# Moving the experts' down-weight loads from SyncE's DMA queue to ScalarE's, in a hybrid decoder step

## The chip, the cores and the metric

One core of one Trainium2 chip runs the whole kernel. The time is device microseconds of one execution, as a median over runs. Engines are TensorE (PE, its weight loads PEld), VectorE (DVE), ScalarE (ACT), GpSimd (POOL) and SyncE (SP). SyncE and ScalarE can each start DMA transfers on a queue of their own; all transfers are carried out by the core's 16 DMA engines.

## The reference

One layer of a decoder for 256 prompt tokens and 8 decode tokens (264 in all, width 1024). Two attention mixers and a merge come first, then the mixture of experts, on which this case turns. Cut to that:

```
def moe_ffn(x, norm_ffn, w_router, b_router, w_gu, b_gu, w_down, b_down):
    xn = rms_norm(x, norm_ffn)
    logits = (xn @ w_router) + b_router
    top_v, top_e = lax.top_k(logits, TOP_K)          # 4 of 32 experts
    gates = jax.nn.softmax(top_v, axis=-1)
...
    def expert_block(args):
        tok, e = args
        h = xn[tok] @ w_gu[e] + b_gu[e]
        gate = jnp.minimum(h[:, :D_FF], SWIGLU_LIMIT)
        up = jnp.clip(h[:, D_FF:], -SWIGLU_LIMIT, SWIGLU_LIMIT)
        return ((up + 1.0) * gate * jax.nn.sigmoid(SWIGLU_ALPHA * gate)) @ w_down[e] + b_down[e]
...
    return x + out                                    # out: the gated sum over each token's experts
```

All is float32. An expert's `w_gu` is 1024 x 2048 (8 MB) and its `w_down` 1024 x 1024 (4 MB), so the 32 experts have 384 MB of weights, each of which is read once.

## The kernel before

The first 340 us or so compute the mixers and the router. Then come the experts, one pass for each, plus one: passes are numbered q = 0 to 32 (`PASSES` = 33, `LAST` = 32). Pass q handles up to 64 tokens of one expert; passes 16 and 17 (`TWICE` and the one behind it) share one expert, which has more tokens, and its gates are multiplied in `gate_up_twice`. The experts' order is decided on the chip and stands in `order_i`; `placed_expert` reads an entry of it into a register (a TENSOR_LOAD).

**On TensorE** (`experts_pe`, `step`): `gate_up(q)` multiplies the pass's tokens by the gate and up weights in four parts (line 1244, 16 matmuls a part); at odd q, after the first part, `scatter` adds the two preceding passes' results (line 1215); `gather(q+1)` picks the next pass's tokens (line 1176); `down(q-1)` multiplies the product of the pass before by the down weights in two halves (line 1326); `turn_rows` (1197) and `turn_product` (1309) transpose. So the down of a pass always runs behind the gate_up of the next.

**Weights in SBUF.** The gate and up weights ("the gates") of a pass are four transfers of 2 MB (line 403), each into a slot of its own; there are four such slots and one early buffer, so that a part of pass q+1 can only be loaded when that part of pass q has been used. The down weights are two halves of 2 MB. There are two sets of slots for them, an even (line 415) and an odd one (lines 409, 411 and 412; its second half is two transfers of 1.5 and 0.5 MB). So the halves for pass q+1 can be loaded when down(q-1) has used its own.

**Semaphores.** `used` counts used gate parts 1 to 3 and `gu` the fourth; `half_down` and `ydone` count first and second halves of down. `gathered`, `clip`, `aturned` and `ydone` release ScalarE's work.

**On SyncE** (`experts_sp`) one queue carries all of it, written out in order: for each q, `load_gate_up(q+1)`, four waits each with a transfer, then `load_down(q+1)`, two waits with two or three transfers. From q = 25 on (`TURN` = 12, line 1715) the order is another: the gates of q+1 go ahead of the downs of q, so that the last entries of the queue are the gates of 32, the downs of 31 and the downs of 32.

**On ScalarE** (`experts_act`, `step`) a pass is `sigmoid(q)` (1383), `keep_rows(q+1)` (a copy of the gathered rows, 1373), `keep_productT(q)` (a copy of the transposed product, 1387) and `keep_out(q-1)` (two copies of the down result into `y`, 1411, on which the next scatter depends). ScalarE starts no transfer in the expert stage; before it, it starts 32 small ones (line 2108).

Of the kernel before, what the change touches and what calls it, by code (L numbers as in the profile page):

```python
# [120 lines left out]
def build(nc, t, const_at, const_w):  # L121
    ctx = ExitStack()
    with ctx:
# [1232 lines left out]
        def load_gate_up(sp, e, done):  # L1356
            for s in range(4):
                if s < 3:
                    sp.wait_ge(S["used"], 3 * done - 2 + s)
                else:  # L1360
                    sp.wait_ge(S["gu"], done)
                load_expert_slot(sp, e, s)

        def load_down(sp, e, done, parity):
            sp.wait_ge(S["half_down"], done)
            load_down_slot(sp, e, 0, parity)
            sp.wait_ge(S["ydone"], done)
            load_down_slot(sp, e, 1, parity)
# [124 lines left out]
        def placed_expert(eng, q):  # L1493
            return eng.value_load(order_i[0:1, bass.ds(q, 1)], min_val=0, max_val=NEXP - 1)
# [190 lines left out]
        def experts_sp(sp):  # L1685
            for s in range(3):
                sp.wait_ge(S["used"], s + 1)
                load_expert_slot(sp, 1, s, turning=False)
            sp.wait_ge(l_listed, 1)
            e = sp.value_load(order_i[0:1, 2:3], min_val=0, max_val=NEXP - 1)  # L1690
            sp.wait_ge(S["gu"], 1)
            load_expert_slot(sp, e, 0)
            for s in range(1, 4):
                sp.wait_ge(S["used"], 3 + s)
                load_expert_slot(sp, e, s)
            load_down(sp, e, 1, 0)
            with sp.Fori(1, TWICE // 2) as k:
                for q, parity in ((2 * k, 1), (2 * k + 1, 0)):
                    e = placed_expert(sp, q + 1)
                    load_gate_up(sp, e, q + 1)  # L1700
                    load_down(sp, e, q, parity)
            e = sp.value_load(order_i[0:1, TWICE + 2:TWICE + 3], min_val=0, max_val=NEXP - 1)
            for s in range(4):
                if s < 3:
                    sp.wait_ge(S["used"], 3 * TWICE + 2 * s + 2)
                else:
                    sp.wait_ge(S["gu"], TWICE + 2)
                load_expert_slot(sp, e, s)
            load_down(sp, e, TWICE, 1)
            with sp.Fori(TWICE // 2 + 1, TURN) as k:  # L1710
                for q, parity in ((2 * k, 0), (2 * k + 1, 1)):
                    e = placed_expert(sp, q + 1)
                    load_gate_up(sp, e, q + 1)
                    load_down(sp, e, q, parity)
            load_gate_up(sp, sp.value_load(order_i[0:1, 2 * TURN + 1:2 * TURN + 2], min_val=0, max_val=NEXP - 1), 2 * TURN + 1)
            with sp.Fori(TURN, PAIRS - 1) as k:
                for q, parity in ((2 * k + 1, 0), (2 * k + 2, 1)):
                    load_gate_up(sp, placed_expert(sp, q + 1), q + 1)
                    load_down(sp, placed_expert(sp, q), q - 1, parity)
            last = sp.value_load(order_i[0:1, LAST:LAST + 1], min_val=0, max_val=NEXP - 1)  # L1720
            load_gate_up(sp, last, LAST)
            load_down(sp, sp.value_load(order_i[0:1, LAST - 1:LAST], min_val=0, max_val=NEXP - 1), LAST - 2, 0)
            load_down(sp, last, LAST - 1, 1)
            sp.wait_ge(l_listed, 3)
            n = listed(sp)
            store_tokens(sp, 0)
            with sp.If(n > 0):
                with sp.Fori(0, n_items) as k:
                    with sp.If(n > k):
                        e = listed_expert(sp, k)  # L1730
                        sp.wait_ge(S["ydone"], k + PASSES)
                        load_gate_up(sp, e, k + PASSES)
                        load_down(sp, e, k + PASSES, 1)
                store_tokens(sp, 6 * n)
                sp.wait_ge(stored["y"], 2 * y_store_count)
            sp.wait_ge(stored["y"], y_store_count)
            for group, count in store_count.items():
                sp.wait_ge(stored[group], count)
# [140 lines left out]
                        pe.wait_ge(t_added, 6 * k + 12)  # L1879

        def experts_act(act):
            def step(q, half, scattered):
                sigmoid(act, q)
                keep_rows(act, q + 1)
                keep_productT(act, q)
                keep_out(act, q - 1, 1 - half, scattered)

            keep_rows(act, 0)
            act.wait_ge(r_shifted, 1)
            nc.scalar.activation(exps, exps, ACT.Exp).then_inc(r_exp, 1)  # L1890
            for q in (1, 2):
                act.wait_ge(r_tail_left, q)
                nc.scalar.copy(tail_parts[0:TAIL, :], tail_rows[0:TAIL, :]).then_inc(r_tail_cast, 1)
            sigmoid(act, 0)
            keep_rows(act, 1)
            keep_productT(act, 0)
            step(1, 1, 0)
            step(2, 0, None)
            with act.Fori(1, TWICE // 2 - 1) as k:
                step(2 * k + 1, 1, k)  # L1900
                step(2 * k + 2, 0, None)
            step(TWICE - 1, 1, TWICE // 2 - 1)
            keep_rows(act, TWICE + 1)
            sigmoid(act, TWICE)
            keep_out(act, TWICE - 1, 1, None)
            keep_productT(act, TWICE)
            sigmoid_again(act, TWICE + 1)
            keep_rows(act, TWICE + 2)
            keep_productT_again(act, TWICE + 1)
            sigmoid(act, TWICE + 2)  # L1910
            keep_rows(act, TWICE + 3)
            keep_out(act, TWICE, 0, TWICE // 2)
            keep_out_again(act, TWICE + 1)
            keep_productT(act, TWICE + 2)
            with act.Fori(TWICE // 2 + 1, PAIRS - 1) as k:
                step(2 * k + 1, 1, k)
                step(2 * k + 2, 0, None)
            step(LAST - 1, 1, PAIRS - 1)
            sigmoid(act, LAST)
            keep_productT(act, LAST, aT_last)  # L1920
            keep_out(act, LAST - 1, 1, None)
            keep_out(act, LAST, 0, PAIRS, bank=BT)
            act.wait_ge(l_listed, 3)
            n = listed(act)
            with act.If(n > 0):
                with act.Fori(0, n_items) as k:
                    with act.If(n > k):
                        m = k + PASSES
                        keep_rows(act, m)
                        sigmoid(act, m)  # L1930
                        keep_productT(act, m)
                        keep_out(act, m, 0, None, k + 1)
# [555 lines left out]
```

## Time and profile before

| what | value |
|---|---|
| median of 3 runs | 1265.12 us (1265.11 to 1266.21) |
| the profiled execution | 1265.79 us, its span 1264.0 us |
| mean granted TensorE clock | 0.999 |
| PE busy | 1220.6 us (97%) |
| DVE, ACT, POOL busy | 377.2, 193.4, 16.1 us |
| bytes by DMA, queue of SyncE | 461.50 MB in 75234 packets |
| bytes by DMA, queue of ScalarE | 1.05 MB in 4608 packets |
| chain that ended last | PE 64%, DMA 28%, SyncE's queue 3%, DVE 3% |

The span runs from the first to the last instruction. Times within the trace are us from its start. "PE busy" counts modelled, overlapping matmuls, so 97% does not mean that TensorE is at its peak. "Idle before" names what an engine had to wait for; "landing" is when a transfer's semaphore has its full count.

### The profile page before, as it was taken

What the parts mean: (1) busy time and instruction counts of PE and PEld (TensorE: products, weight loads), DVE (VectorE), ACT (ScalarE), POOL (GpSimd) and SP (SyncE); (2) the same over time, 40 slices, a digit from 0 to 9 for tenths busy, and PEclk for the clock granted to TensorE, in tenths of its full rate; (3) what the DMA queues carried; (4) which work ended last, traced back from release to release, by engine and by line L of the source; (5) the groups of instructions that cost most, each with busy time, mean ns of one, the idle gap of its engine ahead of it and who ended that gap; (6) DMA issues with size and microseconds to landing.
All of it is one profiled execution on the core that took longest, in us unless ns stands there. A gap on an engine that the chain in (4) does not pass through costs nothing.

```text
span 1264.0 us, 16641 instructions
## 1 busy us (share of the span) xinstructions
PE 1220.6 (97%) x6431; PEld 558.3 (44%) x6431; DVE 377.2 (30%) x924; ACT 193.4 (15%) x438; POOL 16.1 (1%) x28
## 2 busy tenths in 40 slices
PE   9999999999999999999898989999999999999998
PEld 5556678685533443433242333334434333432332
DVE  2555755324433221222121212222212221221223
ACT  3223234301300100110001001101100101000001
POOL 0000000011000000000000000000000000000000
PEclk9999999999999999999999999999999999999999
DMA  9787652498699999999999999999999999999995
GB/s 329 181 244 238 238 162 69 137 335 320 233 428 412 428 427 427 427 428 427 428 428 427 428 427 426 428 422 421 424 427 428 424 431 429 427 429 426 429 424 234
DMA packets 79891, 463.21 MB, mean 366 GB/s; under 512 B 20162, under 2 KB 35290, under 8 KB 54882
## 3 DMA queue, kind: packets, MB, share of 16 engines
q1 hardware_dynamic: 75234, 461.50, 90.3%
q10 hardware_dynamic: 4608, 1.05, 0.5%
q8 instruction: 32, 0.52, 0.2%
q14 instruction: 17, 0.14, 0.0%
HBM read 459.53 MB, written 5.09 MB: 368 GB/s over the span
## 4 chain that ended last, share of the span: by engine, by line
PE 64%; DMA 28%; SPq 3%; DVE 3%; issue 1%; ACT 1%; DVEq 0%; ACTq 0%
PE banks L1244 23%; DMA arena<-w_gu 22%; PE banks L1326 10%; DMA arena<-w_down 5%; PE banks L630 5%; PE banks L2217 4%; PE banks L1215 3%; PE banks L1176 2%; PE banks L810 2%; PE banks L1512 2%; PE banks L1275 1%; PE banks L1197 1%; SPq L263 1%; PE banks L686 1%; PE banks L1224 1%
## 5 line engine op out<-in xcount | busy, mean ns | idle before, releaser
L1244 PE MATMUL banks<-arena 128*64 128x512 f32 x1984 | 442.3, 596 | 23.3 <-DMA arena<-w_gu 22.3
L1244 PEld LDWEIGHTS banks<-arena 128*64 128x64 f32 x1984 | 137.0, 137 | 298.7 <-issue 247.5
L1326 PE MATMUL banks<-arena 128*64 128x512 f32 x1024 | 226.3, 592 | 1.9 <-DMA arena<-w_down 1.9
L1425 DVE TENSOR_SCALAR arena<-banks 128x512 f32<-128x512 f32 x32 | 22.1, 692 | 374.6 <-PE banks L1244 354.2
L1326 PEld LDWEIGHTS banks<-arena 128*64 128x64 f32 x1024 | 72.9, 136 | 136.5 <-issue 125.6
L1383 ACT ACTIVATE arena<-arena 128x512 f32<-128x512 f32 x32 | 20.2, 630 | 537.4 <-DVE arena L1425 537.4
L2217 PE MATMUL banks<-arena 128*128 128x512 f32 (+1 forms) x192 | 78.0, 562 | 0.9 <-ACT arena L2287 0.9
L1466 DVE TENSOR_TENSOR arena<-banks,arena 128x528 f32<-128x528 f32 x64 | 45.3, 708 | 80.8 <-PE banks L1215 80.8
L630 PE MATMUL banks<-arena 128*128 128x264 f32 x256 | 61.7, 396 | 0.5 <-ACT arena L850 0.5
L1176 PE MATMUL banks<-arena 128*64 128x512 f32 x256 | 61.2, 599 | 0.9 <-DVE arena L1418 0.9
L1215 PE MATMUL banks<-arena 128*128 128x264 f32 (+1 forms) x256 | 61.2, 391 | 0.0
L1378 DVE TENSOR_TENSOR arena<-banks,arena 128x512 f32<-128x512 f32 x33 | 22.8, 692 | 123.8 <-PE banks L1197 123.8
L1215 PEld LDWEIGHTS banks<-arena 128*128 128x128 f32 (+1 forms) x256 | 47.0, 189 | 20.5 <-issue 13.0
L1387 ACT COPY arena<-banks 128x512 f32<-128x512 f32 x32 | 18.8, 586 | 221.5 <-PE banks L1309 221.5
L630 PEld LDWEIGHTS banks<-arena 128*128 128x128 f32 x256 | 48.5, 194 | 9.3 <-ACT arena L850 0.9
L2217 PEld LDWEIGHTS banks<-arena 128*128 128x128 f32 x192 | 35.8, 190 | 37.8 <-issue 35.3
L1411 ACT COPY arena<-banks 64x512 f32<-64x512 f32 x64 | 37.1, 580 | 24.2 <-PE banks L1326 23.1
L574 PE MATMUL banks<-arena 128*128 128x285 f32 x128 | 32.1, 410 | 0.0
L1176 PEld LDWEIGHTS banks<-arena 128*64 128x64 f32 x256 | 17.0, 136 | 31.2 <-issue 30.0
L1197 PEld LDWEIGHTS banks<-arena 128*128 128x128 f32 x132 | 18.2, 205 | 27.7 <-issue 23.1
L1421 DVE CAST arena<-arena 96x64 bf16 (+1 forms) x32 | 6.0, 190 | 80.7 <-PE banks L1326 80.7
L810 PE MATMUL banks<-arena 128*128 128x264 f32 x128 | 28.9, 386 | 0.5 <-issue 0.5
(372 smaller groups left out, 923.0 us busy)
## 6 DMA issues: line engine op xcount, KB each, us to landing
arena<-w_gu SPq DMA_DIRECT2D x127, 2048.0 KB, 21.1
arena<-w_down SPq DMA_DIRECT2D x48, 2048.0 KB, 23.6
arena<-w_down SPq DMA_DIRECT2D x16, 1536.0 KB, 23.4
arena<-w_in SPq DMA_DIRECT2D x8, 2048.0 KB, 13.0
arena<-w_down SPq DMA_DIRECT2D x16, 512.0 KB, 24.9
arena<-cache_moba_k SPq DMA_DIRECT2D x16, 256.0 KB, 2.8
arena<-cache_moba_v SPq DMA_DIRECT2D x16, 256.0 KB, 2.8
arena<-w_out SPq DMA_DIRECT2D x2, 2048.0 KB, 13.2
```

Of the source, the lines that this page charges most:

```text
L574: mm = nc.tensor.matmul(banks[:, 4 + 2 * i + m, 0:19 * NC].rearrange("p (s c) -> p s c", c=NC), w1[:, r, P * m:P * m + P], rT[i][:, :, fir ...
L630: mm = nc.tensor.matmul(banks[:, B_GATE, 0:TOK], w[:, c, P * (f % 4):P * (f % 4) + P], xnT[:, c, :], start=(c == 0), stop=(c == KC - 1))
L810: mm = nc.tensor.matmul(banks[:, 4 + 2 * (m % 2) + x, 0:TOK], w[:, j, P * m:P * m + P], o[:, j, :], start=(j == 0), stop=(j == 3))
L1176: nc.tensor.matmul(banks[64 * x:64 * x + 64, BX, :], sel[:, i, :], h[:, i, 512 * x:512 * x + 512], start=(i == 0), stop=False, tile_positi ...
L1197: mm = nc.tensor.transpose(banks[:, BT, P * k:P * k + P], xg[:, first:first + 2 * P - 1:2], ident)
L1215: mm = nc.tensor.matmul(out[:, x, 0:TOK], y[0:rows, 512 * x + P * c:512 * x + P * c + P], selT[0:rows, :], start=True, stop=True)
L1244: mm = nc.tensor.matmul(banks[64 * x:64 * x + 64, BG + b, :], xgT[:, c % 4, 64 * (c // 4):64 * (c // 4) + 64], w[:, D * b + 512 * x:D * b ...
L1326: mm = nc.tensor.matmul(banks[64 * x:64 * x + 64, bank, :], product[:, c, 64 * part:64 * part + 64], w[:, 512 * x:512 * x + 512], start=Fa ...
L1411: nc.scalar.copy(y[64 * half:64 * half + 64, 512 * x:512 * x + 512], banks[64 * x:64 * x + 64, bank, :]).then_inc(S["ykept"], 1)
L1466: nc.vector.tensor_tensor(v, scatter_banks(c)[:, :, 0:TOK], v, ALU.add).then_inc(S["added"], 1)
L1512: mm = nc.tensor.matmul(banks[:, 2 * i + n, :], sig[:, c, P * i:P * i + P], slot((OUT_A, OUT_B)[c // 4], 4)[:, c % 4, 512 * n:512 * n + 51 ...
L2217: mm = nc.tensor.matmul(out, xnT[:, c, P * i:P * i + P], columns(c), start=(c == 0), stop=(c == KC - 1))
```

## The change

The down loads leave SyncE's program. ScalarE's `step` gets them: after `keep_productT(q)` it reads the expert of pass q+1, waits for `half_down` and `ydone` at q, and issues the two halves, and after that it runs `keep_out(q-1)`. Around the double pass the same calls are written out by hand. SyncE's program keeps the gates, pass after pass; the part from `TURN` on goes into one loop with the rest. TensorE's, VectorE's and GpSimd's programs stay as they are, and so do the slots, the bytes and the semaphores' counts.

```diff
@@ experts_sp
-            load_down(sp, e, 1, 0)
             with sp.Fori(1, TWICE // 2) as k:
-                for q, parity in ((2 * k, 1), (2 * k + 1, 0)):
-                    e = placed_expert(sp, q + 1)
-                    load_gate_up(sp, e, q + 1)
-                    load_down(sp, e, q, parity)
+                for q in (2 * k, 2 * k + 1):
+                    load_gate_up(sp, placed_expert(sp, q + 1), q + 1)
...
-            load_down(sp, e, TWICE, 1)
-            with sp.Fori(TWICE // 2 + 1, TURN) as k:
...
-            load_gate_up(sp, sp.value_load(order_i[0:1, 2 * TURN + 1:2 * TURN + 2], min_val=0, max_val=NEXP - 1), 2 * TURN + 1)
-            with sp.Fori(TURN, PAIRS - 1) as k:
-                for q, parity in ((2 * k + 1, 0), (2 * k + 2, 1)):
+            with sp.Fori(TWICE // 2 + 1, PAIRS) as k:
+                for q in (2 * k, 2 * k + 1):
                     load_gate_up(sp, placed_expert(sp, q + 1), q + 1)
-                    load_down(sp, placed_expert(sp, q), q - 1, parity)
-            last = sp.value_load(order_i[0:1, LAST:LAST + 1], min_val=0, max_val=NEXP - 1)
-            load_gate_up(sp, last, LAST)
-            load_down(sp, sp.value_load(order_i[0:1, LAST - 1:LAST], min_val=0, max_val=NEXP - 1), LAST - 2, 0)
-            load_down(sp, last, LAST - 1, 1)
@@ experts_act
-            def step(q, half, scattered):
+            def step(q, half, scattered, parity):
                 sigmoid(act, q)
                 keep_rows(act, q + 1)
                 keep_productT(act, q)
+                e = expert_at_place(q + 1)
+                act.wait_ge(S["half_down"], q)
+                load_down_slot(act, e, 0, parity)
+                act.wait_ge(S["ydone"], q)
+                load_down_slot(act, e, 1, parity)
                 keep_out(act, q - 1, 1 - half, scattered)
...
+            act.wait_ge(l_listed, 1)
-            step(1, 1, 0)
-            step(2, 0, None)
+            step(1, 1, 0, 0)
+            step(2, 0, None, 1)
...
             keep_rows(act, TWICE + 1)
             sigmoid(act, TWICE)
+            e = expert_at_place(TWICE + 2)
+            act.wait_ge(S["half_down"], TWICE)
+            load_down_slot(act, e, 0, 1)
+            act.wait_ge(S["ydone"], TWICE)
+            load_down_slot(act, e, 1, 1)
             keep_out(act, TWICE - 1, 1, None)
...
             keep_out(act, TWICE, 0, TWICE // 2)
+            e = expert_at_place(TWICE + 3)
+            act.wait_ge(S["half_down"], TWICE + 2)
+            load_down_slot(act, e, 0, 0)
+            act.wait_ge(S["ydone"], TWICE + 2)
+            load_down_slot(act, e, 1, 0)
             keep_out_again(act, TWICE + 1)
```

The first place is SyncE's program for pass 2 and the start of the loop behind it. The names are the semaphores; an "ISA" row is a register instruction or a wait. Before:

```order
L403 DMA arena<-w_gu 128x4096
L415 ISA [waits e_half_down]
L415 DMA arena<-w_down 128x4096
L415 ISA [waits e_ydone]
L415 DMA arena<-w_down 128x4096
L1697 UNCONDITIONAL_BRANCH
```

And now:

```order
L403 DMA arena<-w_gu 128x4096
L1696 UNCONDITIONAL_BRANCH
L1696 ISA
L1494 TENSOR_LOAD arena
L1494 ISA x2
```

The fourth gate transfer of pass 2 is followed at once by the loop, which asks for the gates of pass 3.

The second place is ScalarE's program for pass 1. Before:

```order
L1383 ACTIVATE arena<-arena 128x512 [waits e_clip]
L1373 COPY arena<-banks 128x512 [waits e_gathered]
L1387 COPY arena<-banks 128x512 [waits e_aturned]
L1411 COPY arena<-banks 64x512 [waits e_ydone]
L1411 COPY arena<-banks 64x512
```

And now:

```order
L1387 COPY arena<-banks 128x512 [waits e_aturned]
L1869 TENSOR_LOAD arena
L1869 ISA x2
L415 ISA [waits e_half_down]
L415 DMA arena<-w_down 128x4096
L415 ISA [waits e_ydone]
L415 DMA arena<-w_down 128x4096
L1411 COPY arena<-banks 64x512 [waits e_ydone]
L1411 COPY arena<-banks 64x512
```

A register load, two waits and two transfers stand between the copy of the product and the copies of the down result; in odd slots it is three transfers.

## Rows read from the trace of the kernel before

**Rows 1.** The page: GB/s moved by DMA, in 40 equal slices of the span.

```profile
GB/s 329 181 244 238 238 162 69 137 335 320 233 428 412 428 427 427 427 428 427 428 428 427 428 427 426 428 422 421 424 427 428 424 431 429 427 429 426 429 424 234
```

**Rows 2.** Busy time by window: us, PE, PEld, DVE, ACT, POOL, clock, DMA share, GB/s.

```profile
380.00:385.00 5.00, 5.00 (x31) 2.13 (x28) 1.05 (x4) 0.37 (x1) 0.00 (x0) 1.00 0.94 341
...
400.00:1240.00 840.00, 810.60 (x3964) 308.28 (x3962) 185.44 (x369) 87.61 (x153) 0.00 (x0) 1.00 1.01 427
1240.00:1248.00 8.00, 6.91 (x36) 2.52 (x34) 2.49 (x5) 1.93 (x4) 0.00 (x0) 1.00 0.86 361
```

**Rows 3.** Chain of waits, two passes of the middle stage: start us, us, what.

```profile
623.70 25.49 DMA arena<-w_gu
...
682.54 25.49 DMA arena<-w_gu
```

**Rows 4.** Line 403, the gate loads: all of them, then from 540 to 770 us.

```profile
L403 SPq DMA_DIRECT2D arena<-w_gu x127: 327/333/437, 267.0 to 1203.9; - x127
...
DMA to landing us min/median/max: 7.5/21.1/26.1
...
DMA to landing us min/median/max: 23.0/25.5/25.6
```

**Rows 5.** Timeline of SyncE's queue: start us, us, instruction.

```profile
269.44 16.96 SPq L476 DMA_DIRECT2D arena<-b_router  x1
...
344.66 26.84 SPq L403 DMA_DIRECT2D arena<-w_gu  x7
380.18 3.77 SPq L415 DMA_DIRECT2D arena<-w_down  x2
...
852.45 2.06 SPq L415 DMA_DIRECT2D arena<-w_down  x2
```

**Rows 6.** Timeline of ScalarE (ACTq: DMA issues), early, and at pass 1.

```profile
28.50 0.31 ACT L2327 ACTIVATE arena<-arena 128x18 f32<-128x18 f32 x1 [1.24 <-DVE arena L2418]
29.41 1.39 ACTq L2108 DMA_DIRECT2D arena<-cache_nsa_cmp_k  x2
...
384.63 0.59 ACT L1387 COPY arena<-banks 128x512 f32<-128x512 f32 x1 [7.65 <-PE banks L1309]
```

**Rows 7.** Chain of waits, passes 19 to 21, where TensorE does not wait.

```profile
862.92 10.45 PE banks L1244 x48
...
884.58 13.78 PE banks L1244 x64
...
909.09 3.48 PE banks L1244 x16
```

**Rows 8.** Chain of waits around the double pass.

```profile
766.90 3.65 PE banks L1244 x16
...
787.47 3.58 PE banks L1275 x16
...
809.56 6.87 PE banks L1326 x31
...
821.79 3.44 PE banks L1244 x16
...
855.68 3.48 PE banks L1244 x16
```

**Rows 9.** Before the end: timeline of TensorE, then chain of waits.

```profile
1210.42 3.66 PE L1326 MATMUL banks<-arena 128*64 128x512 f32 x16 [0.67 <-DMA arena<-w_down]
...
1215.78 3.43 PE banks L1244 x16
```

**Rows 10.** Timelines of ScalarE and TensorE, start of pass 14.

```profile
722.42 0.59 ACT L1387 COPY arena<-banks 128x512 f32<-128x512 f32 x1 [7.65 <-PE banks L1309]
722.90 1.19 ACT L1411 COPY arena<-banks 64x512 f32<-64x512 f32 x2
...
722.87 3.65 PE L1244 MATMUL banks<-arena 128*64 128x512 f32 x16
```

**Rows 11.** Waits: engine, line, waited for, us in total, times, longest.

```profile
PE banks L1244 <- DMA arena<-w_gu: 22.3, 27, 1.2
```

More of the change, by code:

```diff
@@ L1708, in experts_sp @@
                 load_expert_slot(sp, e, s)
-            load_down(sp, e, TWICE, 1)
-            with sp.Fori(TWICE // 2 + 1, TURN) as k:
[L1711 to L1714, printed above, removed]
-            load_gate_up(sp, sp.value_load(order_i[0:1, 2 * TURN + 1:2 * TURN + 2], min_val=0, max_val=NEXP - 1), 2 * TURN + 1)
-            with sp.Fori(TURN, PAIRS - 1) as k:
-                for q, parity in ((2 * k + 1, 0), (2 * k + 2, 1)):
-                    load_gate_up(sp, placed_expert(sp, q + 1), q + 1)
-                    load_down(sp, placed_expert(sp, q), q - 1, parity)
-            last = sp.value_load(order_i[0:1, LAST:LAST + 1], min_val=0, max_val=NEXP - 1)
-            load_gate_up(sp, last, LAST)
-            load_down(sp, sp.value_load(order_i[0:1, LAST - 1:LAST], min_val=0, max_val=NEXP - 1), LAST - 2, 0)
-            load_down(sp, last, LAST - 1, 1)
+            with sp.Fori(TWICE // 2 + 1, PAIRS) as k:
+                for q in (2 * k, 2 * k + 1):
+                    load_gate_up(sp, placed_expert(sp, q + 1), q + 1)
             sp.wait_ge(l_listed, 3)
@@ L1881, in experts_act, with expert_at_place @@
         def experts_act(act):
-            def step(q, half, scattered):
+            def expert_at_place(p):
+                if isinstance(p, int):
+                    return act.value_load(order_i[0:1, p:p + 1], min_val=0, max_val=NEXP - 1)
+                return placed_expert(act, p)
+            def step(q, half, scattered, parity):
                 sigmoid(act, q)
@@ L1896, in experts_act @@
             keep_productT(act, 0)
-            step(1, 1, 0)
-            step(2, 0, None)
+            act.wait_ge(l_listed, 1)
+            step(1, 1, 0, 0)
+            step(2, 0, None, 1)
             with act.Fori(1, TWICE // 2 - 1) as k:
-                step(2 * k + 1, 1, k)
-                step(2 * k + 2, 0, None)
-            step(TWICE - 1, 1, TWICE // 2 - 1)
+                step(2 * k + 1, 1, k, 0)
+                step(2 * k + 2, 0, None, 1)
+            step(TWICE - 1, 1, TWICE // 2 - 1, 0)
             keep_rows(act, TWICE + 1)
             sigmoid(act, TWICE)
+            e = expert_at_place(TWICE + 2)
[3 more added lines that the diff above has]
+            load_down_slot(act, e, 1, 1)
             keep_out(act, TWICE - 1, 1, None)
@@ L1915, in experts_act @@
             with act.Fori(TWICE // 2 + 1, PAIRS - 1) as k:
-                step(2 * k + 1, 1, k)
-                step(2 * k + 2, 0, None)
-            step(LAST - 1, 1, PAIRS - 1)
+                step(2 * k + 1, 1, k, 1)
+                step(2 * k + 2, 0, None, 0)
+            step(LAST - 1, 1, PAIRS - 1, 1)
             sigmoid(act, LAST)
```

## The prediction

> **What bounds the kernel now.** First the speed of the DMA by slice of the span: from the twelfth slice to the last but one it stands at 412 to 434 GB/s [rows 1]. The windows give the same stretch: from 400 to 1240 us the 16 DMA engines are busy at a share of 1.01, with 427 GB/s at full TensorE clock, and they fall off between 1240 and 1248 us [rows 2]. A share of 0.86 of those 8 us against 1.01 is 6.8 us, so the weights stop coming at about **E = 1246.8 us**. Second, the chain of waits: between 623.70 and 682.54 us two passes go by, 58.84 us [rows 3], in which two experts' weights pass, 12 transfers of 2 MB: **4.90 us a transfer**. TensorE itself needs less: where it does not wait, an odd pass runs 855.68 to 884.58, 28.9 us, and an even one, which has no scatter, 884.58 to 909.09, 24.5 us [rows 7, 8]: 53.4 us a pair. TensorE is busy 97% of the span only because it and the DMA are nearly matched; the matmuls of line 1244 stand idle on w_gu 22.3 us in 27 waits [rows 11]. Third, the queue: in the middle stage a gate transfer takes 25.5 us from issue to landing [rows 4], of which 4.9 are its own. So about four others stand before it, and SyncE is never late. The limit is the number of bytes and **the order in which they come**.
>
> **What the change takes away.** SyncE loses the down loads of 30 passes, 60 waits and 75 issues of about 333 ns each [rows 4]. That is worth nothing: SyncE is not on a path, and its gates are released by TensorE in an order in which no down slot stands in the way, since down(q-1) ends before gate_up(q+1) begins. After the change it is also gone that from pass 25 on SyncE asks for the gates one pass ahead of the downs (`TURN`). This has a price, below.
>
> **What it adds to ScalarE.** Per pass one register load, two or three issues and four or so register instructions. On this engine an instruction behind a waiting one does not overtake it: the copy of 28.50 us waited, and the first DMA behind it comes 0.91 us later, with register load and checks between them [rows 6]. So a down slot is now requested some 0.7 to 0.9 us after the copy of the product begins, and the two waits on down(q-1) are met by then. The copies of the down result, which stood at 722.90, begin about 2 us later (three issues at 0.33 [rows 4], their register work) and end near 726.1. The rows are of the start of pass 14; in an odd pass the scatter that reads these copies follows the first gate part, as 722.87 + 3.65 = 726.5 here [rows 10]. So that costs 0 here, covered by the first part; without that cover it would be 2 us in each of 15 odd passes, though in DMA-bound passes it would vanish. An issue of a large load costs SyncE 0.33 us, so I take that for ScalarE; with the 0.7 of its own small loads (two in 1.39 us [rows 6]) the copies would end 1 us later and the scatter begin up to 0.7 late, still hidden where TensorE waits for the DMA.
>
> **What moves: the order.** No stretch of this trace has two queues full of large loads, so their sharing must be bounded. Ends: the gates get everything first, or the downs do. I take turns of equal packets, half each, the nearest thing to no preference. The Trainium skill (DMA: Bandwidth & Descriptors, "Queues, rings and completion order") has each DMA engine go round-robin between its queues by packets; by that rule the half is right. It stands against the change, too, in "Rules for kernel authors": spreading loads over SyncE and ScalarE gives no bandwidth, only issue time. Row and rule agree that there is little to win: one queue alone already holds a share of 1.01.
>
> *End of the run.* Before, the last DMA wait is for the second down half of pass 30, at 1210.42 [rows 9]; behind it all the gates of 32 had been asked for ahead of four down halves, and TensorE finished from 1210.42 to 1264, 17.2 us after E. After the change down(31) is asked for a pass earlier, and shares with the gates of 31. TensorE then stalls last for the fourth gate part of 31, with 62.9 us of its own still to do: that part, gather, down, turns (the last third of the 10.45 us that end at 873.37 begins at 869.9, and the next pass at 884.58: 14.7 us [rows 7]) and the whole of the last pass (1215.78 to the span's end, 48.2 us [rows 9]). Behind that part on the wire are four gates of 32, two halves of down(32), and of down(31) what is left. From its request TensorE works some 14.5 us and stalls 4 to 5: 3.9 transfers' time, half of it for the two halves; 0.1 to 0.7 of one is left, I take 0.5. So the part lands 6.5 x 4.90 = 31.9 us before the new E, plus 1 us to be seen (the shortest load takes 7.5 us, 2.6 more than 4.90, for both its ends [rows 4]). The end is E - 31.9 + 1 + 62.9 = **E + 32**, against E + 17.2 now: **+14.8**. With the downs all first it would be E + 34.5 (+17.3); with the gates all first E + 24.7 (+7.5).
>
> *A gap at the start.* SyncE issues seven gates from 344.66, 34.3 us of transfers, and at 380.18 the first half of down(2) [rows 5]: just in time, with 341 GB/s for 5 us [rows 2]. ScalarE comes to it only when the product of pass 1 is kept: 384.63 + 0.7 = 385.3. The DMA stands still **5 us** longer (3 to 5.1).
>
> *Gaps at the double pass.* Gate_up_twice and its neighbours take TensorE long while few slots come free. Before, four to five transfers waiting (25.5 us) carry the DMA over it. After, each pass of the DMA-bound stage has its downs landed early, and TensorE stands that much further back. Count: the fourth gate part of pass 15 is behind 59 gates and 27.5 downs from 346 us: 346 + 5 + 86.5 x 4.90 + 1 = 776. From there by the distances of before [rows 8]: pass 16 begins 20.6 later, 796.6; its parts free slots at 802, 807.5, 813 and 818.4; down(15) at 822 and 825.6; pass 18 begins 34.3 later, 830.9; down(19) is asked for 852.45 - 821.79 = 30.7 after that [rows 5, 8], at 861.6; pass 19 begins at 864.8. At 776 the queues hold or soon get 6.5 transfers (to 808), then four gates (to 824.6), down(18) (to 834.4); the gates of 19 start at 835.6, 842.9, 847.8, 852.7 and end at 857.6; down(19) starts at 862.9; down(20) at 895. Gaps: 1.2 + 2.4 + 5.3 + 2.9 = 11.8. Counting on instead, 74 transfers from 895.2 gives E = 1258, which would leave 6 for them. I take **9** (0 to 13). From pass 20 the DMA is late again (67.5 transfers, 331 us, against 306 of TensorE's own passes to the same part), so gaps are lost for good.
>
> **Sum.** E = 1246.8 + 5 + 9 = 1260.8; end 1260.8 + 32 = 1292.8, 28.8 over the span of 1264.0. The profiled execution took 1265.79, 1.8 over its span, and the median of the runs is 1265.12, 1.1 over it: **1294 us**. Bounds: +7.5+3+0 and +17.3+5.1+13 give 1276 and 1300.5. About 0.2% (2.5 us) is what a measurement here tells from no change.
>
> **The rivals.**
> - *Only the order counts* (0.12): the queues never run dry. For it: backlog is deep now. Against: the count above. 1246.8 + 32 + 1.1 = **1280**, range 1276 to 1283.
> - *ScalarE is held at its issues* (0.07). One small issue on SyncE, with large loads before it, lasted 16.96 us [rows 5]. If an issue on ScalarE waits for even one transfer, sigmoid and keep_rows stay in time (the next is 14 us off), but the down copies and with them the scatter are 4.9 us late: 15 odd passes x up to 4.9, less what the DMA-bound ones hide: **1310 to 1340**. Against: its queue holds at most four down halves, and SyncE's issues with more behind them stay at 333 ns, at most 437 [rows 4].
> - *Faster* (0.04): gates no longer stand behind two down halves in one queue; if two queues together carry more than one, the idle time on w_gu of 22.3 us goes [rows 11], and the time is **1243**. It decides only from the rate at which E drops by the 29 us that I count: 29 of 900, over 3%, some 442 GB/s. Against: the share of 1.01.
> - *No difference* (0.03): the same bytes at the same rate, and E sets the end whatever the order: **1265**. Against: the 62.9 us that hang on the last gate part.
>
> **How the numbers follow.** My forecast, order and gaps together, has 0.74, with its own range 1284 to 1303. Slower is 0.74 + 0.12 + 0.07 = 0.93, same 0.03, faster 0.04. The range runs from 1277, the order alone, to 1305, the upper bound with a few us of late scatters; it leaves out the held issues, the two cases at or under 1265 and a small tail.
>
> **What would show it.** The DMA's rate should stay at 427 or 428 where it is busy, with holes of some us near 381, 835 to 863 and 893. The stalls of TensorE should be once a pass, 3 to 5 us, for the fourth gate part, not 1.2 us for several; the last pass should begin near 1244, with 48 us behind it; DMA-to-landing of w_gu should be shorter than 21 us. An issue on ScalarE should be near 0.33 us. I am wrong if the rate with both queues differs by over 1% (9 us), if the first down loads run while ScalarE waits, or if the queues' shares are far from equal in a way that the bounds above miss.

## The result and the profile after

| | before | after |
|---|---|---|
| median of the runs | 1265.66 us | 1299.43 us (1297.82 to 1304.76) |
| profiled execution | 1265.79 us | 1299.16 us |
| its span | 1264.0 us | 1297.3 us |
| mean granted TensorE clock | 0.999 | 0.981 |

The ratio of the two is 1.027, with a 95% interval of 1.0251 to 1.0289: slower, by 34 us. The forecast was 1294 in a range of 1277 to 1305.

The page of the changed kernel: the speed of the DMA by slice, and the two queues.

```profile
GB/s 320 178 249 231 258 137 50 210 319 292 306 343 429 427 427 429 426 429 427 428 428 428 427 428 427 408 336 387 427 428 429 426 428 426 429 427 428 429 386 35
...
q1 hardware_dynamic: 64434, 335.67, 64.9%
q10 hardware_dynamic: 15408, 126.88, 23.6%
```

Against [rows 1] the rate is the same, 426 to 429 GB/s in nearly every slice from the thirteenth on, and there is now a hole in it: two slices at 336 and 387 GB/s, from 843 to 908 us. The two queues, SyncE's (q1) and ScalarE's (q10), carry 335.67 and 126.88 MB. The windows (the last three columns are the granted clock, the DMA's share and GB/s) show where:

```profile
380.00:385.00 5.00, 5.00 (x30) 2.11 (x26) 0.89 (x3) 0.58 (x1) 0.00 (x0) 1.00 0.09 39
400.00:820.00 420.00, 397.37 (x1898) 148.97 (x1896) 87.30 (x177) 42.65 (x72) 0.00 (x0) 0.98 1.01 428
820.00:900.00 80.00, 77.59 (x418) 31.25 (x416) 19.71 (x40) 10.48 (x20) 0.00 (x0) 0.98 0.90 366
860.00:880.00 20.00, 18.71 (x142) 8.97 (x140) 4.13 (x8) 3.19 (x7) 0.00 (x0) 1.00 0.79 324
860.00:865.00 5.00, 3.71 (x62) 1.67 (x62) 0.00 (x0) 1.16 (x2) 0.00 (x0) 1.00 0.26 108
900.00:1240.00 340.00, 320.94 (x1498) 121.03 (x1496) 69.89 (x139) 33.78 (x57) 0.00 (x0) 0.97 1.01 428
1260.00:1264.00 4.00, 4.00 (x24) 1.77 (x22) 1.29 (x2) 0.00 (x0) 0.00 (x0) 1.00 0.46 184
```

The DMA stands nearly still at 380 us, where it had 341 GB/s [rows 2], and has a share of 0.90 around the double pass, from 820 to 900 us (1.00 before), with half of the loss between 860 and 880, most of that in the first five us. E is the time at which the weights stop coming, worked out as in the prediction. From 900 us the DMA is full again at 1.01 and stays so until 1260; a share of 0.46 of the four us behind that is 1.8 us, so E is 1261.8 us, 15.0 later than before. The other 18 us lie behind E. The end of the span is 35.5 us after it, not 17.2.

TensorE's waits for the gates, from its timeline:

```profile
451.41 3.65 PE L1244 MATMUL banks<-arena 128*64 128x512 f32 x16 [0.89 <-DMA arena<-w_gu]
...
483.86 5.35 PE L1244 MATMUL banks<-arena 128*64 128x512 f32 x16 [3.81 <-DMA arena<-w_gu]
...
542.20 5.22 PE L1244 MATMUL banks<-arena 128*64 128x512 f32 x16 [3.02 <-DMA arena<-w_gu]
...
601.50 6.29 PE L1244 MATMUL banks<-arena 128*64 128x512 f32 x16 [4.10 <-DMA arena<-w_gu]
...
659.38 3.65 PE L1244 MATMUL banks<-arena 128*64 128x512 f32 x16 [1.62 <-DMA arena<-w_gu]
```

Before, such a wait of TensorE's on w_gu was 1.2 us at most and there were 27, 22.3 us in all [rows 11]. Now there are 14 in the whole run, most of them once in two passes (483.86, 542.20 and 601.50 are 58 to 59 us apart), nine of them of 3 us or more, and none between 751 and 935 us. Line 403's own view sums them up (who waited: us, times):

```profile
  PE banks L1244: 39.3, 14
...
DMA to landing us min/median/max: 7.6/19.3/29.2
```

So there are fewer waits (14) and longer ones (39.3 us in all). A gate transfer lands sooner after its issue, 19.3 us in the median against 21.1 [rows 4], and still TensorE waits longer for it. And behind a stall of 3 us or more the same 16 matmuls take 5.2 to 6.5 us and not 3.65. Near the end they do so twice more, behind shorter ones:

```profile
1230.59 5.35 PE L1244 MATMUL banks<-arena 128*64 128x512 f32 x16 [2.30 <-DMA arena<-w_gu]
...
1255.14 5.35 PE L1244 MATMUL banks<-arena 128*64 128x512 f32 x16 [0.80 <-DVE arena L1466]
```

The granted clock in those places explains it, four us at 0.57 each, between them 1.00:

```profile
1231.00:1235.00 4.00, 4.00 (x14) 1.19 (x12) 0.00 (x0) 0.00 (x0) 0.00 (x0) 0.57 0.98 418
1235.00:1255.00 20.00, 19.34 (x96) 8.29 (x92) 7.05 (x12) 2.96 (x5) 0.00 (x0) 1.00 1.01 428
1255.00:1259.00 4.00, 3.86 (x10) 1.18 (x12) 0.08 (x1) 0.00 (x0) 0.00 (x0) 0.57 0.99 419
```

A mean of 0.57 over four us is 3.4 us at half: the clock is at 1.2 GHz there and not 2.4, and the part behind it takes 1.7 us longer. Both stretches lie behind the last wait for the DMA, where nothing hides them.

The adding up of the results (the scatter, line 1215), which depends on ScalarE's copies, was not held up. TensorE sat idle before it for 0.0 us in the whole run (the last number):

```profile
L1215 PE MATMUL banks<-arena 128*128 128x264 f32 (+1 forms) x256 | 61.2, 391 | 0.0
```

### The profile page after: what moved, and what is told of

It is laid out like the page before. It is cut to its first block, busy times and chain, and to the rows that moved or that the text cites. A ratio compares the mean times of both kernels' runs of the same rounds, so it can differ in the third digit from the quotient of the medians.

```text
span 1297.3 us, 16737 instructions
## 1 busy us (share of the span) xinstructions
PE 1237.8 (95%) x6431; PEld 564.6 (44%) x6431; DVE 379.6 (29%) x924; ACT 194.8 (15%) x439; POOL 16.0 (1%) x28
## 3 DMA queue, kind: packets, MB, share of 16 engines
q1 hardware_dynamic: 64434, 335.67, 64.9%
q10 hardware_dynamic: 15408, 126.88, 23.6%
## 4 chain that ended last, share of the span: by engine, by line
PE 63%; DMA 29%; DVE 3%; SPq 3%; issue 1%; ACT 1%; ACTq 0%; DVEq 0%
DMA arena<-w_gu 28%; PE banks L1244 24%; PE banks L1326 9%; PE banks L630 4%; PE banks L2223 4%; PE banks L1215 3%; PE banks L1176 2%; PE banks L810 2%; PE banks L1512 2%; PE banks L1275 1%; PE banks L1197 1%; SPq L263 1%; PE banks L686 1%; DVE arena L919 1%; DVE arena L917 1%
## 5 line engine op out<-in xcount | busy, mean ns | idle before, releaser
L1244 PE MATMUL banks<-arena 128*64 128x512 f32 x1984 | 462.2, 620 | 40.3 <-DMA arena<-w_gu 39.3
L1244 PEld LDWEIGHTS banks<-arena 128*64 128x64 f32 x1984 | 143.6, 142 | 327.7 <-issue 272.6
L1326 PE MATMUL banks<-arena 128*64 128x512 f32 x1024 | 225.4, 592 | 0.0
L1326 PEld LDWEIGHTS banks<-arena 128*64 128x64 f32 x1024 | 73.2, 136 | 133.4 <-issue 128.0
L1176 PE MATMUL banks<-arena 128*64 128x512 f32 x256 | 61.2, 599 | 0.9 <-DVE arena L1418 0.9
L1176 PEld LDWEIGHTS banks<-arena 128*64 128x64 f32 x256 | 16.9, 136 | 31.5 <-issue 30.3
L1197 PEld LDWEIGHTS banks<-arena 128*128 128x128 f32 x132 | 18.2, 205 | 28.2 <-issue 23.1
## 6 DMA issues: line engine op xcount, KB each, us to landing
arena<-w_gu SPq DMA_DIRECT2D x127, 2048.0 KB, 19.3
arena<-w_down ACTq DMA_DIRECT2D x15, 1536.0 KB, 21.9
arena<-w_down ACTq DMA_DIRECT2D x15, 512.0 KB, 27.6
```

What stands on the lines that cost most here:

```text
L1176: nc.tensor.matmul(banks[64 * x:64 * x + 64, BX, :], sel[:, i, :], h[:, i, 512 * x:512 * x + 512], start=(i == 0), stop=False, tile_positi ...
L1197: mm = nc.tensor.transpose(banks[:, BT, P * k:P * k + P], xg[:, first:first + 2 * P - 1:2], ident)
L1244: mm = nc.tensor.matmul(banks[64 * x:64 * x + 64, BG + b, :], xgT[:, c % 4, 64 * (c // 4):64 * (c // 4) + 64], w[:, D * b + 512 * x:D * b ...
L1326: mm = nc.tensor.matmul(banks[64 * x:64 * x + 64, bank, :], product[:, c, 64 * part:64 * part + 64], w[:, 512 * x:512 * x + 512], start=Fa ...
```

## The experiments

Where two traces are compared closely, the measure is the expert stage, from the first matmul of line 1244 to the end of the trace: 923.0 us before (from 341.0) and 956.7 us after (from 340.6), 33.7 apart. It leaves out the attention stage, in which the profiled executions of three experiments (3, 4 and 9) had a granted clock of 0.61 from 146 to 168 us, where before had 0.92; they began the experts 7 to 10 us late, and each was the slowest of its four.

**1. One queue, natural order.** SyncE carries all again, but does not turn the order at pass 25: the first loop runs on to the end, and the turned part behind it is taken out.

```diff
-            with sp.Fori(TWICE // 2 + 1, TURN) as k:
+            with sp.Fori(TWICE // 2 + 1, PAIRS) as k:
                 for q, parity in ((2 * k, 0), (2 * k + 1, 1)):
                     e = placed_expert(sp, q + 1)
                     load_gate_up(sp, e, q + 1)
                     load_down(sp, e, q, parity)
...
```

> The kernel before, with all loads on SyncE's queue, but without the turn at pass 25: after the gates of q+1 come the downs of q+1 in every pass. My theory (the order of the bytes decides the end, and there are no gaps): the weights stop at 1247 us as before, since nothing is requested later, but two down halves of pass 31 now stand ahead of the gates of 32 and no longer behind them, 2 x 4.90 us: 1275 us (1272 to 1277), DMA at 427 GB/s throughout. Rival A (the loss comes only from the second queue or from ScalarE): 1266, no change. Rival B (losing the turn is all of the loss): 1299.

Measured: 1275.29 us, ratio 1.0078 (1.0038 to 1.0119), span 1273.4. Its windows, and its last wait for the DMA:

```profile
380.00:385.00 5.00, 5.00 (x30) 2.06 (x26) 0.61 (x2) 0.00 (x0) 0.00 (x0) 1.00 0.90 338
860.00:880.00 20.00, 20.00 (x95) 8.07 (x96) 6.26 (x11) 1.22 (x2) 0.00 (x0) 1.00 1.00 427
1240.00:1260.00 20.00, 18.91 (x98) 7.17 (x96) 6.06 (x10) 2.38 (x4) 0.00 (x0) 1.00 0.37 154
```

```profile
1210.46 3.65 PE L1244 MATMUL banks<-arena 128*64 128x512 f32 x16 [0.15 <-DMA arena<-w_gu]
```

No gap, and E = 1240 + 20 x 0.37 / 1.01 = 1247.3, as before to within 1 us. The last wait is for the fourth gate part of pass 31, and from there to the end are 62.9 us. So losing the turn is worth **9.6 us by itself** (1275.29 against 1265.66; 9.4 between the two spans, and 5 to 15 by the interval of the ratio), with one queue and no change to ScalarE. Rivals A and B fall.

**2. The same, with requests as late as ScalarE's.** SyncE waits for the copy of the product before it asks for the downs, except around the double pass, where its requests stay as they were.

```diff
+                    sp.wait_ge(S["atkept"], q + 1)
                     load_down(sp, e, q, parity)
```

> The same, and SyncE asks for the downs of q+1 only when the product of pass q is kept, as ScalarE does in the change, save around the double pass. One queue, so no sharing. My theory: a gap of 4 to 5 us at 380 us, as in the change, and small ones behind the double pass, since requests come some 5 us later and the DMA has no other work there: E = 1252 to 1256, time 1280 to 1285. What is then left to the change's 1299 is the sharing of the two queues (downs that overtake gates). Rival A (sharing costs nothing, late requests and the lost turn are all): 1296 to 1300. Rival B (late requests are hidden by the queue): 1275, as without them.

Measured: 1284.61 us, ratio 1.015 (1.0115 to 1.0184), span 1283.0.

```profile
380.00:385.00 5.00, 5.00 (x28) 1.89 (x23) 0.19 (x1) 0.00 (x0) 0.00 (x0) 1.00 0.36 154
860.00:880.00 20.00, 20.00 (x100) 8.82 (x98) 4.66 (x9) 2.04 (x5) 0.00 (x0) 1.00 0.85 342
1240.00:1260.00 20.00, 19.20 (x101) 8.08 (x99) 8.07 (x13) 0.63 (x1) 0.00 (x0) 1.00 0.86 360
```

```profile
1219.68 3.65 PE L1244 MATMUL banks<-arena 128*64 128x512 f32 x16 [0.17 <-DMA arena<-w_gu]
```

The gap at 380 us is there, and so is the one behind the double pass, on one queue. E = 1240 + 20 x 0.86 / 1.01 = 1257.0, 9.7 later and 1.0 above what was expected, and the time 9.3 longer: **on one queue, late requests are worth 9 us**. Rival B falls, and so does rival A, which had all of the loss here. What is left to the change is 14.8 us. Not all of that need be the sharing of two queues: around the double pass the change asks later than this run does, and loses more there (a share of 0.79 against 0.85 from 860 to 880 us). Its expert stage is 941.2 us (from 341.8). No stretch of half clock falls into it before TensorE's last matmuls, and no wait of TensorE on the DMA exceeds 1.3 us.

**3. ScalarE asks before it copies the product.**

```diff
                 keep_rows(act, q + 1)
-                keep_productT(act, q)
                 e = expert_at_place(q + 1)
...
                 load_down_slot(act, e, 1, parity)
+                keep_productT(act, q)
                 keep_out(act, q - 1, 1 - half, scattered)
```

> The change, but in step() ScalarE asks for the two down halves ahead of the copy of the product, so that it waits for the slots themselves. Requests come when the slots are free, 4.4 us earlier for the first half and 1 us for the second. My theory: the gap at 380 us closes to about 1 us and those behind the double pass shrink by 1 or 2 us, and the rest stays: E near 1256, time 1293 to 1296. Rival A (the gaps are worth nothing, or the copies of ScalarE are what is late): 1299. Rival B (ScalarE, held in waits, delays TensorE): 1300 or more.

Measured: 1298.01 us, ratio 1.0236 (1.0202 to 1.027); the profiled execution was the slowest of four and began its expert stage at 350.8, 10 us late. By the stage, 952.2 us, 4.5 less than the change. In its windows, which are to be read 10 us later than the change's:

```profile
390.00:395.00 5.00, 5.00 (x30) 2.26 (x28) 0.99 (x4) 0.52 (x2) 0.00 (x0) 1.00 0.91 328
830.00:910.00 80.00, 77.59 (x426) 31.39 (x424) 18.94 (x39) 10.37 (x20) 0.00 (x0) 1.00 0.93 378
```

The first gap is closed (0.91, against 0.09 in the change and 0.94 before [rows 2]). Around the double pass the share is 0.93 for 0.90, 2.4 us in 80, so those gaps shrink too. The weights stop at 1260 + 20 x 0.31 / 1.01 = 1266.1 (a share of 0.31 from 1260 to 1280), which is 915.3 us into the stage against 921.2 in the change: 5.9 sooner, as the theory had it. But the last wait on w_gu comes only 2.6 us sooner (887.4 us into the stage against 890.0), and 1.7 of the 4.5 is clock, since the part behind the 0.8 us on VectorE takes 3.65 us here. The theory's times did not come: the median, 1298.01, lies above its 1293 to 1296 and within 1 us of rival A's 1299, and the runs (1294.04 to 1304.78) can't tell the two apart. So a gain in time is not shown; what is shown is that the gaps close.

**4. Down loads with rows of 8 KB.** Each half goes in two or three transfers; the semaphores' counts follow. (Shown is `odd_first`; the other slots are split likewise.)

```diff
-                eng.dma_start(odd_first, src).then_inc(ring_in[RING], 16)
+                for c in (0, 2):
+                    eng.dma_start(odd_first[:, c:c + 2, :], src[:, c:c + 2, :]).then_inc(ring_in[RING], 16)
```

> The change, with each down half in two transfers whose rows are 8 KB instead of one with rows of 16 KB (the last third of the odd ones 4 KB). Gates stay at 16 KB. Theory of sharing packet by packet: a down load gets a third of the DMA where gates are queued too, not half; its landings slow from 14 us after the request to some 20 or more for the second piece, the gates' quicken, the stalls of TensorE for the fourth gate part shrink, and the time falls to 1280 to 1292 although no byte less is moved and ScalarE issues twice as much. Rival A (queues share by bytes or by transfer): landings of the pieces as before (first 7 to 9 us, both by 14), time 1299. Rival B (more issues on ScalarE cost): 1301 to 1305.

Measured: 1292.12 us, ratio 1.0191 (1.0154 to 1.0228), at the upper edge of the 1280 to 1292 expected; the expert stage is 947.9 us, 8.8 less than the change's. Line by line of its DMA issues (KB each, us to landing):

```profile
arena<-w_gu SPq DMA_DIRECT2D x127, 2048.0 KB, 16.9
arena<-w_down ACTq DMA_DIRECT2D x105, 1024.0 KB, 28.2
```

The gates land sooner, 16.9 us against 19.3, and the down pieces of half the size take 28.2 instead of 14.0. Rivals A and B fall: what a queue gets goes by the size of its packets (ScalarE's queue has 24048 of them for its 126.89 MB, 15408 in the change). The 28.2 us are not all transfer. By my estimate a third of the rate takes 2 x 4.90 x 3 = 29.4 us for the downs of a pass, which is the length of a pass (58.84 / 2), so a piece often stands behind those of the pass before. The price of the other extreme shows too: now TensorE waits for downs, once for 8 us.

```profile
647.43 6.21 PE L1329 MATMUL banks<-arena 128*64 128x512 f32 x16 [8.08 <-DMA arena<-w_down]
```

**5 and 6. The change in one half of the run only.** `act_first`: ScalarE loads up to pass 16, then SyncE as before, with the turn. `act_second`: SyncE up to pass 16, then ScalarE.

The same condition stands in both:

```diff
+            def step(q, half, scattered, parity):
...
+                if parity is not None:
+                    e = expert_at_place(q + 1)
```

> ScalarE loads the downs for passes 2 to 16 only; from the double pass on SyncE's queue carries all as before, the turn at pass 25 with it. My theory: the gap at 380 us (5 us) and that behind the double pass stay, so E is some 10 to 11 us later, and the end of the run is as before, E + 17: 1276 (1273 to 1279). Rival (the loss accumulates in every pass in which two queues share): half of the change's 34 us, 1282 or more.

> The other half: SyncE's queue carries all up to pass 16, ScalarE the downs from pass 18 on, in natural order. My theory: no gap at 380 us and a small one at most behind the double pass, since the queue comes there as full as before: E 1247 to 1249; the end of the run is the change's, E + 36: 1284 to 1288. With act_first's extra 10 that makes the change's 34. Rival (every pass with two queues costs): 1282 or less, and both halves alike.

Measured: `act_first` 1278.73 us, ratio 1.0082 (1.0054 to 1.0111); `act_second` 1288.06 us, ratio 1.0173 (1.0128 to 1.0218). Against 1266.25 us of before in the same runs that is 12.5 and 21.8, together 34.3: the change's loss, in two parts that add. That they agree within 1 us is partly luck, since the intervals reach 4 us to either side for the first and 6 for the second. The windows of the first, then of the second:

```profile
380.00:385.00 5.00, 5.00 (x26) 1.92 (x23) 0.22 (x2) 0.00 (x0) 0.00 (x0) 1.00 0.35 147
860.00:880.00 20.00, 18.71 (x142) 9.01 (x140) 4.12 (x8) 3.20 (x7) 0.00 (x0) 1.00 0.82 331
1240.00:1260.00 20.00, 18.91 (x100) 7.67 (x100) 7.35 (x12) 1.22 (x2) 0.00 (x0) 1.00 1.00 424
```

```profile
380.00:385.00 5.00, 5.00 (x30) 2.14 (x28) 0.89 (x3) 0.82 (x2) 0.00 (x0) 1.00 0.95 338
880.00:900.00 20.00, 20.00 (x102) 7.37 (x100) 3.00 (x7) 2.38 (x4) 0.00 (x0) 1.00 0.89 361
1240.00:1260.00 20.00, 18.12 (x94) 6.87 (x93) 8.20 (x14) 0.63 (x1) 0.00 (x0) 1.00 0.50 210
```

And the last wait of the second on a gate part:

```profile
1218.22 3.65 PE L1244 MATMUL banks<-arena 128*64 128x512 f32 x16 [0.93 <-DMA arena<-w_gu]
```

`act_first` has both gaps (147 and 331 GB/s) and weights that come until 1260, 13 us later than before, and its span ends at 1277.0, 17 us behind them, as before: its loss is all gaps, some 2 us more of them than expected. `act_second` has neither gap at these places, but one at 880 to 900 us, and E = 1249.9, 3.1 later than before. Its span ends at 1281.5 (this execution took 1283.33 us, 4.7 less than the median), 31.6 us behind E, which is 14.4 more than before. The E + 36 that was expected is the change's own; here the part behind the last wait takes 3.65 us and the clock stays at full speed up to the last matmuls. By the spans the halves cost 13.0 and 17.5 us, 30.5 together, and the change 33.3; two stretches of half clock (3.4 us), which this execution of `act_second` does not have behind its last wait, are about what is missing. The rival with a loss in every pass would have both halves alike, which they are not, though 1278.73 lies only 2.7 above the theory's centre and 3.3 below the rival's bound.

**7. Filling the stall.** Four matmuls into a bank that is free, before the wait for the fourth gate part, in passes 19 to 31. TensorE first waits until the bank has been read.

```diff
+                def filled(c):
+                    if c == 5:
+                        pe.wait_ge(S["ykept"], 2 * (q - 1))
+                        if scattered is not None:
+                            pe.wait_ge(S["added"], 4 * scattered + 5)
+                        keep_warm(fill, BY)
```

> The change, and in passes 19 to 31 TensorE runs four matmuls of 0.53 us into a bank that is free, ahead of its wait for the fourth gate part, where it stood idle 2 to 4 us. Their results are overwritten and used by nobody. Theory (the stall lets the granted clock fall to half for 3.4 us, and that makes the fourth part 5.35 us instead of 3.65): the half-clock stretches after 900 us are gone, and since only the last two lie behind the last DMA wait, the time falls by twice 1.7: 1296 (1295 to 1297). Rival (the clock costs nothing that the DMA does not hide): 1299. Rival (the filling itself delays TensorE): 1300 to 1303.

Measured: 1318.62 us, ratio 1.0424 (1.0372 to 1.0477). The third rival, and beyond its bound. I had the matmuls at half their length. From its chain of waits:

```profile
990.70 3.48 PE banks L1244 x16
...
1004.96 3.63 PE banks L1502 x8
1008.59 3.58 PE banks L1244 x16
...
1051.67 3.48 PE banks L1244 x16
```

The fill takes 3.63 us and the part behind it 3.58, at full clock; a pair of passes becomes 61 us (990.70 to 1051.67), more than the DMA's 58.8, with nothing but TensorE's own work in the chain, and TensorE is the limit. The run says nothing on the price of the clock, and was repeated with half the fill.

**8. Two matmuls, and the change once more beside it.**

> filled_stall with two filling matmuls a pass instead of four. Four took 3.63 us in its trace, 0.9 each, and made a pair of passes 61 us, over the 58.8 of the DMA, so TensorE became the limit; two take 1.8 and make 57.0. Theory (half the clock for 3.4 us behind a stall costs 1.7 us, twice behind the last DMA wait): no half-clock stretch between 900 us and the last pass, or few, and the time 3 us under the change's, 1296; measured from the first gate matmul to the end of the trace 953 to 954 against 956.7. Rival (the clock costs nothing here): 956 to 957. Rival (filling delays again): over 957.

> The change itself once more, on the chip of filled_two, for the comparison: 1299 (1297 to 1301), 956 to 957 us from the first gate matmul to the end of the trace, with some seven half-clock stretches after 900 us. If filled_two saves the 3 us, the two stand 3 us apart; if the clock costs nothing, they are equal.

Measured: 1299.05 us (ratio 1.0249, 1.0213 to 1.0286) and 1298.03 us (1.0228, 1.0194 to 1.0263). No difference in time. The last waits of TensorE, of `filled_two` and then of `change_again`:

```profile
1234.00 3.65 PE L1244 MATMUL banks<-arena 128*64 128x512 f32 x16 [1.24 <-DMA arena<-w_gu]
...
1256.86 3.65 PE L1244 MATMUL banks<-arena 128*64 128x512 f32 x16 [0.80 <-DVE arena L1466]
```

```profile
1231.90 5.35 PE L1244 MATMUL banks<-arena 128*64 128x512 f32 x16 [2.32 <-DMA arena<-w_gu]
...
1256.46 5.29 PE L1244 MATMUL banks<-arena 128*64 128x512 f32 x16 [0.80 <-DVE arena L1466]
```

Here the two prices part. From the last wait to the end are 1296.8 - 1234.00 = 62.8 us with the fill and 1298.3 - 1231.90 = 66.4 without: the half clock costs 3.6 us there (two parts of 5.35 and 5.29 us for 3.65 make 3.3 of them), and the fill gives it back. But the last wait itself comes later (892.9 us into the stage against 890.2), so by the stage 955.7 stands against 956.6. My reading, which no run here singles out, is that the fill holds TensorE up and slots come free later. Theory and rival both hold in part: the clock does cost 3.6 us, and this way of avoiding it gains 0.9 by the stage and nothing in the medians.

**9. Early requests and 8 KB rows together.** The edits of 3 and 4.

> Both mendings of the two-queue form together: requests ahead of the product copy, and down loads in rows of 8 KB, so that the gates get two thirds. In the two traces of these alone the stage from the first gate matmul to the end took 952.2 and 947.9 us against the change's 956.7. If they add: 943.4, which is 1286 to 1287. If the full queue keeps the DMA from running dry it may be less, 1276 to 1282. No theory has it below the kernel before, 1266, as the downs still come ahead of their turn.

Measured: 1293.41 us (1284.69 to 1299.46), ratio 1.0185 (1.0119 to 1.0251), expert stage 948.0 us (from 349.5). They do not add: 4.5 and 8.8 would have made 943.4, and together they give 8.7. In this run and in 4 TensorE's last wait for the DMA is for a down half (2.93 us until 1189.19, and 3.90 us until 1186.15), where in the change it is for a gate part. It stays 27 us above the kernel before. No experiment came below that kernel.

## Why the prediction was right

- **Bound and rate.** Right. The share of the DMA stays at 1.01 from 900 to 1240 us with two queues. The rival with more bandwidth has nothing in any run, which agrees with what the Trainium skill says in DMA: Bandwidth & Descriptors, "Rules for kernel authors".
- **E.** Forecast 1260.8, measured 1261.8. The gap at the start was put at 5 us; the change has 0.09 for 0.94 in five us, 4.2, and 1.0 more from 385 to 400 us. For those at the double pass I chose 9: from 820 to 900 us the DMA's share is 0.90 against 1.00, 8 us, and some 2 us of the 15.0 are not placed. The schedule behind the count holds: pass 18 began at 831.95 (forecast 830.9), pass 19 at 867.53 (864.8), down(19) was asked for at 864.47 (861.6), and the largest hole, forecast at 857.6 to 862.9, is there from 860 to 865. The 9 itself was a choice between two counts, 11.8 and 6, and that it came so near is partly luck.
- **End of the run.** The last wait was forecast at E - 30.9 and came at 1230.59, E - 31.2. Behind it I had 62.9 us of TensorE's work; `filled_two` has 62.8, but the change 66.7. **The term that was too small is this one**, by 3.8 us, of which 3.4 are two stretches of half clock at 1.7 us each; no row of before showed one in the experts, and the prediction had none. That is most of the 5 us between 1294 and 1299. The order itself is the term of 14.8, and `act_second`, whose trace has no half clock behind the last wait, has 14.4.
- **TensorE's stalls.** Forecast once a pass, 3 to 5 us, for the fourth gate part. There were 14 in the run and not some 30, nine of them over 3 us. The last was 2.30 us, where the sum for the end took a stall of 4 to 5; that E - 31.2 came so near to E - 30.9 all the same is partly luck.
- **Sharing in halves.** Right for loads with rows of 16 KB, as most are; the two transfers with shorter rows got less than half. The change's own trace shows it. An odd pass's three down transfers are issued within 1 us (ScalarE's timeline):

```profile
410.76 0.58 ACT L1387 COPY arena<-banks 128x512 f32<-128x512 f32 x1 [7.66 <-PE banks L1309]
411.45 0.35 ACTq L409 DMA_DIRECT2D arena<-w_down  x1
411.96 0.34 ACTq L411 DMA_DIRECT2D arena<-w_down  x1
412.46 0.34 ACTq L412 DMA_DIRECT2D arena<-w_down  x1
412.84 1.18 ACT L1411 COPY arena<-banks 64x512 f32<-64x512 f32 x2 [1.49 <-issue]
```

and land (KB each, median us to landing) as follows:

```profile
arena<-w_down ACTq DMA_DIRECT2D x45, 2048.0 KB, 14.0
arena<-w_down ACTq DMA_DIRECT2D x15, 1536.0 KB, 21.9
...
arena<-w_down ACTq DMA_DIRECT2D x15, 512.0 KB, 27.6
```

The 2 MB half lands after 13.8 us (line 409 alone): 9.8 at half the rate and 2.6 for the ends, which leaves 1.4 open. The 1.5 MB one has rows of 12 KB beside the gates' 16. Taking turns it gets 12/28, so its 3.7 us become 8.6; measured (411.96 + 21.9) - (411.45 + 13.8) = 8.6. The last has rows of 4 KB, 4/20, so 1.23 us become 6.1; measured (412.46 + 27.6) - (411.96 + 21.9) = 6.2. With experiment 4 this is shown, and it agrees with the round-robin by packets that the Trainium skill states (DMA: Bandwidth & Descriptors, "Queues, rings and completion order").
- **ScalarE held.** Didn't happen: its issues last 0.34 to 0.37 us. The copies of the down result begin at 412.84, 2.1 us after the product's copy, as worked out, and end before the scatter at 414.8. The first request comes at 384.93, forecast for 385.3.

- **How the 34 us divide.** The forecast put 14.8 on the order of the end and 14 on gaps. `act_first` and `act_second` bear that out: 13 us of gaps in the one, 14.4 of order and 3.1 of gap in the other, and the half clock on top. Experiments 1 and 2 divide it another way: the lost turn 9.6, late requests 9.3, two queues and what else the change has 14.8. These add because each is the difference of two neighbouring runs, and another sequence of steps could give other prices: on two queues early requests took 4.5 off the stage. The last is, from the spans of experiment 2 and the change, 14.3: E 4.8 later (1257.0 to 1261.8), the last wait nearer to it (37.3 us before E, then 31.2: the downs of 31 came ahead of its gates), 6.1, and 3.4 of clock. What was wrong in the text is a shade: it named the turn and the overtaking as one price. The turn is worth 9.6 even with one queue.

What stays open: why the two mendings of experiments 3 and 4 do not add (no form with two queues throughout came below 947.9 us), how much of the 14.8 is the later asking around the double pass, and what decides whether a stall is followed by the lower clock.

## What to carry to other kernels

Where the DMA is full, as it was here at a share of 1.01, a transfer on a second queue is not free and not faster: it takes its share from the transfers that are needed first. One queue in the order of need is then a schedule, and its order at the very end (what is loaded last, and how much work hangs on it) was worth 9.6 us here. A load that is moved to a busy engine is also requested when that engine gets round to it, which costs once the queue has run low (9.3 us here); and loads that come before they can be used made the consumer's stalls fewer and longer (14 for 27, 39.3 us for 22.3), with 3.4 us of clock on top.

## What was not expected of the hardware

- In the changed kernel's rows above, waits of TensorE of 0.89 and 1.62 us are followed by a part of 3.65 us, those of 2.30 and 3.02 to 4.10 us by one of 5.22 to 6.29 us, at half the clock. But `act_early` has waits of 2.64 and 3.25 us with 3.65 us behind them. So the length of the wait alone does not tell.
- The gap of 0.8 us on VectorE in the last pass was harmless before (the part behind it 3.65 us) and came with half the clock in the change (5.35), 24 us after a longer wait; in `filled_two`, without that, it was 3.65 again. But it was 3.65 in `act_early` too, 24 us after a wait of 2.96 us, so the longer wait before it doesn't tell either.
- The share of a queue follows the size of its packets closely enough to time transfers by it: 8.6 for 8.6 and 6.2 for 6.1 us.
